# Weighing the index scores two heads at a time on GpSimd

## The reference

```
s = einsum('bthd,bsd->bths', qi, ki)                  # 8 index heads of 32
score = einsum('bth,bths->bts', wi, relu(s))          # weighted sum over the 8 heads
score = where(visible, score, -inf)
top_val, top_idx = top_k(score, top_k)                # then attention over the keys picked
```

## Time and profile before

| what | value |
|---|---|
| median of three runs | 3309.23 us |
| the profiled execution: its time, its span | 3313.95 us, 3312.1 us |
| TensorE matmul busy | 3009.8 us (91%) |
| VectorE busy | 2047.0 us (62%) |
| ScalarE busy | 1163.4 us (35%) |
| GpSimd busy | 1246.4 us (38%) |
| line 1001 on GpSimd | 80 operations, 252.8 us, mean 3160 ns |

### The profile page before, as it was taken

The page is one execution under the profiler, slowest core; times in us unless marked ns, Lnnn a source line. Parts: engine busy times, 40 slices in busy tenths (PEclk is TensorE's granted clock), DMA queues, the critical chain, the costliest instruction groups (busy, mean ns, idle before and its releaser), DMA issues. The chain is left out here.

```text
span 3312.1 us, 49478 instructions
## 1 busy us (share of the span) xinstructions
PE 3009.8 (91%) x18794; PEld 2835.4 (86%) x18794; DVE 2047.0 (62%) x3899; ACT 1163.4 (35%) x2031; POOL 1246.4 (38%) x470
## 2 busy tenths in 40 slices
PE   7999985787888789998999999998898999999997
PEld 5888864676877678897999999998788999999996
DVE  5656653878787887423666566665216666766664
ACT  4333334676777666522121211111212211222112
POOL 0000003677788772044533333432145333433320
PEclk7999996999999999998999999999999999999998
DMA  4222225321211100232111111111322111111101
GB/s 167 87 85 85 106 75 150 85 61 38 55 38 31 28 25 25 81 90 71 39 63 51 38 38 38 51 51 52 105 65 77 39 38 38 51 53 48 38 13 54
DMA packets 166244, 200.47 MB, mean 61 GB/s; under 512 B 27967, under 2 KB 140900, under 8 KB 164068
## 3 DMA queue, kind: packets, MB, share of 16 engines
q1 hardware_dynamic: 165076, 198.81, 18.6%
q10 hardware_dynamic: 1040, 0.00, 0.0%
HBM read 153.53 MB, written 45.25 MB: 60 GB/s over the span
## 5 line engine op out<-in xcount | busy, mean ns | idle before, releaser
L1001 POOL TENSOR_TENSOR keep_long<-keep_long,keep_w 128x2048 f32<-128x2048 f32 (+10 forms) x80 | 252.8, 3160 | 709.7 <-ACT keep_long L1158 709.7
L1827 DVE SCALAR_TENSOR_TENSOR ffn_gv<-ffn_up,ffn_taps,ffn_gv 128x1056 f32<-128x1056 f32 (+2 forms) x264 | 415.0, 1586 | 157.5 <-ACT ffn_gv L1780 151.2
L1848 DVE TENSOR_TENSOR feed_hT<-feed_hT,ffn_ps_d 128x352 f32<-128x352 f32 x528 | 275.0, 521 | 329.1 <-PE ffn_ps_d L1733 329.1
L1720 PE MATMUL ffn_ps_u<-feed_nhi,feed_up_hi 128*128 128x352 f32 x2112 | 460.1, 326 | 15.5 <-DVE feed_nlo L1858 11.0
L1720 PE MATMUL ffn_ps_u<-feed_nhi,feed_up_lo 128*128 128x352 f32 x2112 | 456.6, 324 | 0.0
L1720 PE MATMUL ffn_ps_u<-feed_nlo,feed_up_hi 128*128 128x352 f32 x2112 | 456.4, 324 | 0.0
L1720 PEld LDWEIGHTS ffn_ps_u<-feed_nhi,feed_up_hi 128*128 128x128 f32 x2112 | 360.9, 190 | 19.0 <-DVE feed_nlo L1858 12.4
L1733 PE MATMUL ffn_ps_d<-ffn_a_hi,ffn_down_hi 128*128 128x352 f32 x1056 | 343.5, 325 | 23.7 <-DVE ffn_a_lo L1839 18.3
L1720 PEld LDWEIGHTS ffn_ps_u<-feed_nhi,feed_up_lo 128*128 128x128 f32 x2112 | 364.0, 188 | 0.0
L1720 PEld LDWEIGHTS ffn_ps_u<-feed_nlo,feed_up_hi 128*128 128x128 f32 x2112 | 360.1, 188 | 0.0
L1106 PEld LDWEIGHTS att_ps_o<-att_v,att_pT 128*128 128x128 f32 x2176 | 285.4, 196 | 81.6 <-ACT att_pT L914 67.1
(11 more groups left out here) (253 smaller groups left out, 6011.6 us busy)
## 6 DMA issues: line engine op xcount, KB each, us to landing
feed_raw_up<-in_w_up SPq DMA_DIRECT2D x44, 1024.0 KB, 4.9
scratch_sT<-keep_long SPq DMA_DIRECT2D x16, 1472.0 KB, 5.1
ffn_raw_down<-in_w_down SPq DMA_DIRECT2D x22, 1024.0 KB, 4.8
feed_nlo<-scratch_mixT SPq DMA_DIRECT2D x16, 528.0 KB, 6.6
keep_short<-in_x_prompt SPq DMA_DIRECT2D x16, 512.0 KB, 4.8
att_qa<-scratch_sT SPq DMA_DIRECT2D x16, 512.0 KB, 4.9
att_qb<-scratch_sT SPq DMA_DIRECT2D x32, 256.0 KB, 5.5
feed_raw_up<-in_w_out SPq DMA_DIRECT2D x16, 512.0 KB, 3.8
```

The lines of the kernel that those rows point to most:

```text
L1001: st.step(pool.tensor_tensor(at, at, weights, ALU.mult))
L1720: ins = pe.matmul(ps_u[:, half, s, 0:SUB], a[:, q, k, :], b[:, k, SUB * s:SUB * s + SUB], start=(k == 0 and n == 0), stop=(k == KC - 1 and ...
L1827: ins = dve.scalar_tensor_tensor(gv[:, half, lo:hi], up[:, lo + shift + j - 2:hi + shift + j - 2], taps[:, 2 * j + half, e:e + 1], gv[:, h ...
L1848: dve.tensor_tensor(at, at, ps_d[:, j % 2, 0:SUB], ALU.add).then_inc(partial_read[j % 2], 1)
```

## The change

Each operation over four heads becomes two over two heads. The first weighing of a pair waits only for the relus of its two heads. The last two operations (two heads by two, one by one) stay. Between the two operations of a pair there is no wait for the first one's end; the step or the count stands on the second.

```
-                pool.wait_ge(relu_ready, 4 * group + 4)
-                weights = keep["w8"][0:b.T, b.n, 4 * half:4 * half + 4].unsqueeze(2).broadcast_to([b.T, 4, w])
-                st.step(pool.tensor_tensor(at, at, weights, ALU.mult))
+                for h in (0, 2):
+                    pool.wait_ge(relu_ready, 4 * group + h + 2)
+                    weights = keep["w8"][0:b.T, b.n, 4 * half + h:4 * half + h + 2].unsqueeze(2).broadcast_to([b.T, 2, w])
+                    ins = pool.tensor_tensor(at[:, h:h + 2], at[:, h:h + 2], weights, ALU.mult)
+                st.step(ins)
...
-                    pool.tensor_tensor(last_four, first_four, last_four, ALU.add).then_inc(paired, 1)
+                    for h in (0, 2):
+                        ins = pool.tensor_tensor(last_four[:, h:h + 2], first_four[:, h:h + 2], last_four[:, h:h + 2], ALU.add)
+                    ins.then_inc(paired, 1)
```

## The result

The changed kernel takes 3261.11 us in the median (3260.03 to 3262.92, four runs), the kernel before 3307.89 in the runs beside it: a ratio of 0.9856, 95% interval 0.9844 to 0.9868, so 46.8 us or 1.4% faster. The forecast was 3291 us with 3274 to 3308. The direction was right. The gain is two and a half times the one forecast (18 us), and the time lies outside the range.

The account below looks back on a forecast made before the run. The attention phase was taken as bound by engine hand-offs, with VectorE blocked by GpSimd. Path -16.5, clock -3, added work +1 give -18.5 us on 3313.95, so 3295.5; with the runs' median 4.7 lower, 3291 us, range 3274 to 3308.

Parts of the forecast that it names:

- What bounds the kernel: Attention phase, 870 us: no engine full; VectorE sits out GpSimd operations on a shared port, delaying ScalarE, then TensorE.
- The time sat out: Five VectorE lines blocked until GpSimd operations end: 86 us in all, of which 33 us would go.
- the sum of squares: If VectorE arrives at random, blocking follows squared GpSimd operation lengths per segment: 54.1 before, 33.3 after, ratio 0.62.
- The share on the path: Half of the 33 us won on VectorE, 16.5 us, was taken to shorten the kernel; ends 3 and 33 us.
- the finer start: First weighing of a pair can start two relus earlier, taking about 1.8 us off a segment's end where GpSimd waited.
- The clock: TensorE's granted clock drops after idle time; less of this was to save 3 us, ends 0 and 11 us.
- One avoided dip: Six microseconds of TensorE at clock 0.54 cost 2.8 us of full-speed work; one taken as avoided, for 3 us.
- What it adds: Three more GpSimd operations per segment, 24 us less 5 us at seams, mostly hidden; 1 us charged.
- hold the port as one: Rival: a pair's second GpSimd operation takes the port before VectorE gets in; 4 us lost, 3313 us, chance 0.12.
- waited away: Rival: VectorE's time won goes into waits for TensorE or new meetings; gain 0 to 6 us, 3306 us, chance 0.13.
- become the last: Rival: GpSimd's added work delays `paired`, holding up ScalarE's relus, then TensorE; +10 us, 3319 us, chance 0.10.

Follow-up runs that it names:

- off_port_before: Kernel before with GpSimd untouched, operands of lines 1247 and 1270 laid out in groups of three to keep off the shared port: 3261.3 us, ratio 0.9856.
- late_start: Changed kernel, but the first weighing of a pair waits for all four relus as before: 3272.2 us, ratio 0.9892 to the kernel before.
- add_split: Kernel before with only the addition of four heads halved, weighings whole: 3290.0 us, ratio 0.9948.
- weigh_split: Kernel before with only the weighings halved, each with its finer wait, addition of four heads whole: 3283.0 us, ratio 0.9924.
- off_port_after: Changed kernel with lines 1247 and 1270 also laid out off the shared port: 3254.2 us, ratio 0.9836 to the kernel before.
- one_head: Changed kernel with weighings and additions of the halves cut to one head, 14 GpSimd operations per segment: 3253.2 us, ratio 0.9829 to the kernel before.
- off_port_three: Changed kernel with lines 1230, 1247 and 1270 laid out off the shared port: 3246.1 us, ratio 0.9810 to the kernel before.
- gpsimd_extra: Changed kernel with one more GpSimd multiplication of 192 elements per segment: 3263.2 us, ratio 0.9862 to the kernel before.
- seam_wait: Changed kernel with GpSimd waiting for the first operation of each pair before the second: 3263.1 us, ratio 0.9865 to the kernel before.

## Why the prediction was wrong in size and right in its mechanism

- *What bounds the kernel*: right. VectorE sitting out whole GpSimd operations, passed on through ScalarE to TensorE, is the cost; `off_port_before` shows it without touching GpSimd.
- *The time sat out*: near. 33 of 86 us should have gone, 40.4 did. The sum of squares took VectorE's arrivals as random, and for line 1247 they were not: it came close behind the starts of GpSimd's operations before and no longer did after, so that its time sat out fell from 28.5 us to 4.2. The prediction had no term for that, and as far as these runs show it was luck. Lines 1230 and 1278 did worse than the sum of squares.
- *The share on the path*: the first step that failed. It was put at a half, 16.5 us. TensorE's idle time fell by 32.6 us, which is 0.8 of the 40.4. In the kernels without the finer start the same division gives 0.62 to 0.66 (`late_start` 24.7 of 39.8, `off_port_before` 37.2 of 56.4, `add_split` 19.2 of 30.0). With it the division gives 0.81, 0.73 (`weigh_split`) and 0.72 (`off_port_after`), but 0.66 in `one_head`. So the half was too low for the holds alone, and part of the rest may belong to the finer start, which the prediction counted only as cover for GpSimd's added work and gave no gain of its own; without it the kernel is 11 us slower (3272.2 and 3261.1). Whether the start itself does it stays open, as said above. VectorE's 122.3 us of waiting for TensorE were read as slack that would swallow gains; they came to 129.6 us, so 7 us of the gain went there. Line 1230, set aside as hidden, is worth 8 us in `off_port_three`.
- *The clock*: the second step that failed, by about as much. One avoided dip, 3 us, was put in; TensorE's busy time fell by 18.7 us. The upper end considered, four dips and 11 us, was too low as well. The earlier trace rows priced one dip and none was counted: there are ten of 0.78 or less between 602 and 1100 us before and three after. The clock of 0.93 over the phase in the earlier trace rows was a sign of more than one dip, though it does not give the gain by itself: much of the lost clock lies in idle time or in the first 100 us, which lose the same in both kernels.
- *What it adds*: right in its price and too small in its size. 24 us of GpSimd less 5 was the sum, and the busy time rose by 28.8 us; between 900 and 1000 us GpSimd was 92.73 busy, where 87 had been worked out. 1 us was charged for it; `gpsimd_extra` puts 22.2 us of such work at about 2, within the uncertainty.
- *The rivals*: the pair does not hold the port as one (the place at 952.49 us, and `seam_wait`). Of the time won by VectorE a fifth was waited away, 7 us of 40.4. GpSimd did not become the last, not even at 97.89 busy between 900 and 1000 us in `one_head`, near the point that was set for that rival.

From the 18.5 us of the forecast to the 51.3 of the profiled executions, the misses are: 3.7 us for the time sat out (7.4 more, at a half), 12.4 for the share (0.81 in place of 0.5, of 40.4), 15.7 for the clock and 1 for the added work. Even the upper ends of the prediction, 33 and 11 us, would not have reached it.

## What to carry to other kernels

A tiny VectorE operation with a long median is a sign of a held port: compare the shortest with the median, and look which GpSimd operation ends with it. Two cures work and overlap: cut GpSimd's operations, since their length and hardly their number counts while others have to sit them out, or lay out VectorE's small operands so that they keep off the port, which adds no operation to GpSimd. When such a stall ends in an idle TensorE, count the clock dips of the phase and add their price; here the fall of TensorE's busy time was more than a third of the gain.

## What the runs showed of the hardware

- An operation of nine numbers per partition was held for up to 4.3 us in the kernel before and never in the other layout (163 ns in the median, `off_port_before`): whether it is held depends on the layout of the operands, however few they are. The 31 operations of lines 1230, 1247 and 1270 that took over 0.28 us in the kernel before all ended 0.02 to 0.04 us behind the end of a GpSimd operation.
- A waiting VectorE operation got in at the seam between two GpSimd operations although the second one waited for nothing, in seven places of the changed kernel, and a wait between the two brought nothing (`seam_wait`, 3263.1 and 3261.1 us).
- Cutting a GpSimd operation costs little here. An addition of 2048 elements takes 4.55 us and two of 1024 take 2 x 2.43, which is 0.31 more; a multiplication of two inputs over 192 elements takes 554 ns.
